# Reordering the loads and the plan of an eight-core transformer-layer kernel on Trainium2

## The reference, cut to what matters

```python
h   = modulate(layer_norm(x), mod_x[0], mod_x[1])          # mod = silu(c) @ w_ada + b_ada
q, k, v, u, vb, ga, gb = split(h @ w_in)
ya  = window_attention(rope(q), rope(k), v, kc, vc, sink)  # +-128 tokens, and 256 context keys
vn  = layer_norm(gelu(vb), gmlp_ln_g, gmlp_ln_b)           # per chunk of 128 tokens:
yb  = gelu(u) * (w_s @ vn + b_s)
mix = (sigmoid(ga) * (ya @ w_a) + sigmoid(gb) * (yb @ w_b)) @ w_o
x_mid = layer_norm(ALPHA * x + mod_x[2] * mix)             # then a SwiGLU FFN, and a second norm
```

## Time and profile before

| | us |
|---|---|
| median of 3 runs | 969.98 |
| lowest and highest run | 969.21, 974.94 |
| the profiled execution, slowest core and what lies around it | 974.86 |
| span of its slowest core (core 6) | 973.1 |
| PE busy in that span | 890.9 |

### The profile page before, as it was taken

One profiled execution on the slowest core, in us unless ns is written; L12 is line 12 of the kernel. 1 busy time (PEld: TensorE's weight loads), 2 busy tenths in 40 slices (PEclk: granted clock), 3 DMA queues, 4 the chain that ended last, 5 costly groups with the idle time before them and its releaser, 6 DMA issues.

```text
span 973.1 us, 15750 instructions; the slowest of 8 cores (966.4 to 973.1 us)
## 1 busy us (share of the span) xinstructions
PE 890.9 (92%) x5495; PEld 446.2 (46%) x5589; DVE 622.9 (64%) x1131; ACT 317.7 (33%) x494; POOL 284.6 (29%) x231
## 2 busy tenths in 40 slices
PE   1389688898999999999999999999999999999995
PEld 1235444344554444444444544444444444444673
DVE  4337686857655666766687476556656674666787
ACT  1436775546867243334435200111111001011110
POOL 6024263555554233324312540202202021111111
PEclk9999898979999999999999999999999999999999
DMA  8997622339963500026321480303213020111112
GB/s 203 202 187 190 174 87 66 88 46 161 164 95 81 174 1 1 1 88 100 114 47 44 173 192 25 87 1 87 36 52 87 0 44 1 44 44 57 52 66 87
DMA packets 30380, 83.91 MB, mean 86 GB/s; under 512 B 2912, under 2 KB 3168, under 8 KB 28640
## 3 DMA queue, kind: packets, MB, share of 16 engines
q0 software_dynamic: 18064, 34.54, 22.9%
q1 hardware_dynamic: 12240, 48.37, 14.2%
HBM read 109.05 MB, written 8.39 MB: 121 GB/s over the span
## 4 chain that ended last, share of the span: by engine, by line
PE 84%; DMA 6%; DVE 4%; issue 3%; ACT 2%; POOL 1%; DVEq 0%; POOLq 0%; SPq 0%; ACTq 0%
PE psum L1178 31%; PE psum L1204 15%; PE psum L1016 11%; PE psum L1033 6%; PE psum L1067 6%; DMA arena<-wqk 4%; PE psum L673 3%; PE psum L729 3%; PE psum L900 2%; PE psum L936 2%; PE psum L760 2%; DMA arena<-ctxb 1%; DVE arena L495 1%; PE psum L1102 1%; DVE arena L974 1%
## 5 line engine op out<-in xcount | busy, mean ns | idle before, releaser
L1178 PE MATMUL psum<-arena 128*128 128x512 bf16 (+1 forms) x1515 | 314.5, 361 | 1.1
L1178 PEld LDWEIGHTS psum<-arena 128*128 128x128 bf16 x1536 | 150.2, 98 | 154.5
L1184 ACT ACTIVATE arena<-psum 128x512 f32<-128x512 f32 (+1 forms) x96 | 53.9, 562 | 380.4 <-PE psum L1178 380.4
L1204 PE MATMUL psum<-arena 128*128 128x512 bf16 x681 | 161.0, 379 | 1.9 <-DVE arena L1187 0.7
L508 POOL TENSOR_TENSOR arena<-arena 128x1 f32<-128x1 f32 (+1 forms) x74 | 70.9, 958 | 287.2 <-DVE arena L506 272.0
L1218 DVE TENSOR_TENSOR arena<-arena,psum 128x512 f32<-128x512 f32 x224 | 140.5, 679 | 18.8 <-PE psum L1204 18.6
L1187 DVE TENSOR_TENSOR arena<-psum,arena 128x512 bf16<-128x512 f32 (+1 forms) x96 | 62.0, 646 | 131.2 <-PE psum L1178 127.8
L1016 PE MATMUL psum<-arena 128*128 128x512 bf16 x498 | 115.7, 379 | 1.4 <-issue 1.0
L495 DVE BATCH_NORM_STATS2 arena<-arena 128x6 f32<-128x512 f32 x152 | 99.7, 685 | 14.5 <-DMA arena<-xh 3.8
L1204 PEld LDWEIGHTS psum<-arena 128*128 128x128 bf16 x704 | 68.6, 98 | 82.7 <-issue 2.6
L906 ACT ACTIVATE arena<-psum 128x1024 bf16<-128x1024 f32 (+1 forms) x100 | 80.7, 852 | 23.2 <-PE psum L900 22.1
(11 more groups left out here) (95 smaller groups left out, 883.2 us busy)
## 6 DMA issues: line engine op xcount, KB each, us to landing
arena<-xh SPq DMA_DIRECT2D x34, 512.0 KB, 7.7
arena<-wada POOLq DMA_DIRECT2D x24, 512.0 KB, 18.0
arena<-wff POOLq DMA_DIRECT2D x11, 1024.0 KB, 9.2
arena<-wff SPq DMA_DIRECT2D x11, 1024.0 KB, 7.0
out<-arena SPq DMA_DIRECT2D x15, 512.0 KB, 2.6
arena<-wc POOLq DMA_DIRECT2D x8, 768.0 KB, 20.0
arena<-wout SPq DMA_DIRECT2D x8, 512.0 KB, 4.4
arena<-rope SPq DMA_DIRECT2D x4, 512.0 KB, 11.5
```

What stands on the lines that cost most here:

```text
L1178: ins = e.matmul(bank(ps)[:, 0:n], lhsT=w1v[r][:, k, lo:lo + 128], rhs=h2(k), start=(k == 0), stop=(k == 7))
L1184: s = P.op('act', prio - 150, act_cost(n), lambda e: e.activation(out=sgv(), in_=bank(pg)[:, 0:n], func=AF.Silu), after=[a], takes=[sg], g ...
L1204: ins = e.matmul(bank(ps), lhsT=actv[(r, fi, t)], rhs=w2v[r][:, fi, h * 512:(h + 1) * 512], start=(n == 0), stop=(n == 2 * len(rounds) - 1))
```

## The change: loads moved, a lag and costs raised, one wait added

It does this:

- The `w_ada` pieces 8 to 11 are no longer loaded behind `wvvb` into four buffers. Their loads wait for the second tile of group 3 and have two buffers.
- Tile buffers: two more, in the part of `qg` that belongs to group 3. Group 3's tiles may use them. (Buffers 6 and 7 of `a4` lie in the same place; pieces 8 to 11 no longer use them, so q and u of group 3 need not wait for those pieces.)
- The first rotation table is loaded behind piece 5 of `w_ada`. All that stands behind it on SP's queue follows it.
- The bias product on PE waits for the table `bsbc`.
- `LAG` of POOL goes from 0.12 to 1.2, and some costs go up, so that the whole order is made anew.
- A DVE instruction (`t_shut`) is added, whose result nothing reads: the branches `MASKPE` and `ZPOOL` are off.

```diff
-    LAG = {'pe': 0.24, 'act': 0.10, 'dve': 0.10, 'pool': 0.12, 'sp': 0.1}
+    LAG = {'pe': 0.24, 'act': 0.10, 'dve': 0.10, 'pool': 1.2, 'sp': 0.1}
...
-    o_xr = [o_wo + 4 * KB * i for i in range(4)] + [L['qg'] + 8 * KB, L['qg'] + 12 * KB, L['vn'] + 4 * KB]
+    o_xr = [o_wo + 4 * KB * i for i in range(4)] + [L['qg'] + 8 * KB, L['qg'] + 12 * KB, L['vn'] + 4 * KB,
+                                               L['qg'] + 24 * KB, L['qg'] + 28 * KB]
...
-    rope_load('0', 14, rope_d[0], 512, [])
+    rope_load('0', 14, rope_d[0], 512, [ada_ld[5]])
...
-            res.append(P.op('pool', prio - 40, (hi - lo) / 512.0 * 1.1 + 0.2, ...
+            res.append(P.op('pool', prio - 40, (hi - lo) / 512.0 * 1.3 + 0.2, ...
...
-            t_vn[j] = P.op(me, prio + i - 20, 0.75 if me == 'dve' else 1.3, ...
+            t_vn[j] = P.op(me, prio + i - 20, 0.9 if me == 'dve' else 1.5, ...
...
-    m1 = P.op('pe', 58, 0.7, fgl, after=[c1, c2, ld_wst], takes=[pg], gives=[gh])
+    m1 = P.op('pe', 58, 0.7, fgl, after=[c1, c2, ld_wst, ld_bsbc], takes=[pg], gives=[gh])
...
+    shut = V(U0 + 46 * KB, BF16, 4, 128)
+    t_shut = P.op('dve', 58.5, 0.4, lambda e: e.tensor_scalar(
+        out=shut, in0=masks, scalar1=-1.0, scalar2=1e30, op0=ALU.add, op1=ALU.mult), after=[ld_masks, c2])
...
-    norm_group('3', [xh[(13 + i) * 128:(14 + i) * 128, :] for i in range(4)], 64, [ld_wu[1]])
+    ld_x3 = norm_group('3', [xh[(13 + i) * 128:(14 + i) * 128, :] for i in range(4)], 64, [ld_wu[1]], ('act', 'act'), room=(7, 8, 0, 1, 2, 3))
...
-        ada(8 + n, [(2, 2 * n), (2, 2 * n + 1)], 30 + n, (0, 1, 6, 7), after=[ld_wvvb])
-    ada_mid = ada_last[8:]
+        ada(8 + n, [(2, 2 * n), (2, 2 * n + 1)], 30 + n, (0, 1), after=[ld_x3[1]])
...
-    proj_qk(3, 108, ada_mid)
-    proj_u(3, 110, ada_mid)
+    proj_qk(3, 108)
+    proj_u(3, 110)
...
-                ex = P.op(me, prio + n * 0.1, 1.0 if me == 'dve' else 2.1, ...
+                ex = P.op(me, prio + n * 0.1, 1.1 if me == 'dve' else 2.2, ...
...
-        t_yb[j] = P.op('dve', prio + 0.9, 0.8, ...
+        t_yb[j] = P.op('dve', prio + 0.9, 0.98, ...
```

More of the change, by code:

```diff
@@ L772, in proj_v @@
             r, st = stat(prio + i, [gvs], 512, [[ge]], EPS)
-            mi = minus(st, prio + i - 20, r)
-            z = P.op('act', prio + i - 20, 0.82, lambda e, st=st, gvs=gvs: e.activation(
-                out=gvs(), in_=gvs(), func=AF.Identity, scale=rstd_of(st), bias=minus_of(st)), after=[mi], gives=[st])
             me = 'dve' if i % 2 == 0 else 'pool'
-            t_vn[j] = P.op(me, prio + i - 20, 0.75 if me == 'dve' else 1.3, lambda e, gvs=gvs, j=j: e.tensor_tensor(
+            if me == 'dve' or not ZPOOL:
+                mi = minus(st, prio + i - 20, r)
+                z = P.op('act', prio + i - 20, 0.82, lambda e, st=st, gvs=gvs: e.activation(
+                    out=gvs(), in_=gvs(), func=AF.Identity, scale=rstd_of(st), bias=minus_of(st)), after=[mi], gives=[st])
+            else:
+                z = P.op('pool', prio + i - 20, 1.0, lambda e, st=st, gvs=gvs: e.tensor_scalar(
+                    out=gvs(), in0=gvs(), scalar1=mean_of(st), scalar2=rstd_of(st), op0=ALU.subtract, op1=ALU.mult),
+                    after=[r], gives=[st])
+            t_vn[j] = P.op(me, prio + i - 20, 0.9 if me == 'dve' else 1.5, lambda e, gvs=gvs, j=j: e.tensor_tensor(
                 out=vn[:, j, :], in0=gvs(), in1=glg, op=ALU.mult), after=[z, ld_gl, busy], gives=[gv])
@@ L892, in attend @@
             ptv = lambda pt=pt: V(o_pt[sid(pt)], BF16, 8, 128)
+            mi = None
+            if kd == 'w' and s != 1:
+                mi = (0 if j == 0 else 1) if s == 0 else (3 if j == NT - 1 else 2)
             ex = []
@@ L900, in f @@
                         ins = e.matmul(b[:, i * 512:(i + 1) * 512], lhsT=ks[x * 64:(x + 1) * 64, :],
-                                       rhs=qv[x * 64:(x + 1) * 64, :, jt * 128:(jt + 1) * 128], start=True, stop=True)
+                                       rhs=qv[x * 64:(x + 1) * 64, :, jt * 128:(jt + 1) * 128], start=True, stop=mi is None)
+                        if mi is not None:
+                            ins = e.matmul(b[:, i * 512:(i + 1) * 512], lhsT=ident,
+                                           rhs=shut[:, mi:mi + 1, :].to_broadcast([128, 4, 128]), start=False, stop=True)
                     return ins
-                mm = P.op('pe', prio + n * 0.1, 0.2 * len(kv), f, after=need + tile_q(j),
+                mm = P.op('pe', prio + n * 0.1, 0.42 if mi is not None and j < MASKPE else 0.2 * len(kv), f, after=need + tile_q(j) + ([t_shut] if mi is not None and j < MASKPE else []),
                           behind=[s_last, gelus[(1, 2, 3)[min(j // 2, 2)]]], takes=[sp])
@@ L911, in attend @@
             exps.append(mm)
-            if kd == 'w' and s != 1:
-                mi = (0 if j == 0 else 1) if s == 0 else (3 if j == NT - 1 else 2)
+            if mi is not None and j < MASKPE:
+                shut_done.append(mm)
+            elif mi is not None:
                 me = 'dve' if s == 2 and j >= 4 else 'pool'
-                ex = P.op(me, prio + n * 0.1, 1.0 if me == 'dve' else 2.1, lambda e, ptv=ptv, mi=mi: e.tensor_tensor(
+                ex = P.op(me, prio + n * 0.1, 1.1 if me == 'dve' else 2.2, lambda e, ptv=ptv, mi=mi: e.tensor_tensor(
                     out=ptv(), in0=ptv(), in1=masks[:, mi:mi + 1, :].to_broadcast([128, 8, 128]), op=ALU.mult),
```

19 lines of the change are left out of this document (12 added, 7 removed).

## The result

Beside one another on the same chips the changed kernel took 968.07 us and the kernel before 974.07, medians of 20 runs each; the ratio is 0.9944 [0.9931, 0.9957], 5.4 us less. The forecast was 9.6 less (960.4; range 951 to 972), counted from 969.98, the median of the 3 runs known then. In the profiled execution of the changed kernel, 968.28 us, core 7 is the slowest, with a span of 966.5.

What follows compares the result with a forecast made beforehand. PE was taken to bound the kernel, with gains only where it stands still or runs at 1.2 GHz; -7.6 - 1.0 - 1.0 = -9.6 us took 969.98 to 960.4, range 951 to 972.

Steps and rivals of the forecast that it cites:

- Gate pieces, -7.6: 97 to 117 us: with gate loads moved away, context tiles and `bsbc` land 7 us earlier; net -7.6 us.
- rival 3: Tiles don't come sooner, as when the plan holds back their buffers by the lag: 970 us; chance 0.03.
- The margin and the raised costs, 0: POOL's raised lag and costs only reorder the engines; 0 us, bounds -8 and +21.
- Rival 1: The new order is better after 117 us too: a further -8 us, 952; chance 0.16.
- Rotation tables, -1.0: Start, up to the first projection at 52.28: tables behind piece 5 spare `w_ada` pieces; -1.0 us net.
- Two tile buffers, -1.0: Two of group 3's tiles come ten us sooner, their statistics falling into DVE's idle time; -1.0 us.
- Bias wait, 0: PE's bias product waits in the open for `bsbc`; 0 us, range 0 to +1.8.
- gate pieces late, 0: Later gate pieces end near 119 us, 13 us of cover before `w_out` at 131.78; cost 0.
- Rival 2: From 117 us DVE can't keep up and takes back 6 to 7 us: 967; chance 0.17.
- Rival 4: Slower: raised lag puts POOL's masks and rotation sums on more DVE products, 117 to 240 us: 982; chance 0.10.

Runs made afterwards that it cites:

- 10: Changed kernel with two more buffers for normed copies, for the halo group alone; 0.9934 of the kernel before.
- run 12: Changed kernel with two of the halo group's four normed copies allowed on DVE instead of ACT; 1.0003 of the kernel before.
- run 3: Changed kernel with POOL's old lag of 0.12, raised costs kept; 0.9902 of the kernel before.
- run 7: Changed kernel with POOL's lag of 1.2 on all steps but the norms' powers, which have 0.12; 0.9943 of the kernel before.
- run 6: Changed kernel with POOL's lag of 1.2 only behind the norms' powers, 0.12 elsewhere; 0.9939 of the kernel before.
- run 4: Changed kernel with the four gate pieces issued early again, beside the halo and context tiles; 0.9991 of the kernel before.
- run 2: Changed kernel with old lag and old costs: moved loads, tile buffers and the bias product's wait kept; 0.9932 of the kernel before.
- run 1: Kernel before with only POOL's lag raised from 0.12 to 1.2; 0.995 of the kernel before.
- run 16: Kernel before with only the four raised costs of the change; 1.0014 of the kernel before.
- run 14: Changed kernel with POOL's lag at 0.12 and the bias product without its wait for its table; 0.9936 of the kernel before.
- run 9: Changed kernel with POOL's lag at 1.5 instead of 1.2; 0.9942 of the kernel before.
- 13: Changed kernel with POOL's lag at 0.12 and two of the halo group's four normed copies allowed on DVE; 0.9989 of the kernel before.
- 8: Changed kernel with POOL's lag at 0.6 instead of 1.2; 0.9915 of the kernel before.

## Why the prediction missed, step by step

**Gate pieces, -7.6: the step that failed.** "So the second context tile lands near 95.1 instead of 102.1, 7 us earlier" took the issue as given at 91.29 and the best time on the way, 3.8 us, for the rest. In the changed kernel it is issued at 91.74 and takes 6.35 us, so of the 3.0 us that are missing 2.5 lie on the way and 0.5 in the issue; with the lag off it is issued at 89.88 and takes 6.43, landing at 96.31. When it is issued hangs on ACT's copies of group 2, which I hadn't looked at: that is a part of the condition of rival 3, to which I gave 0.03. Then "moved up by 7 us they let the halo projection begin near 107 ..., so I leave 1.5 us of standstill". It moved by 4.0 us, just as the tile did, but the idle time before it was 5.87 + 1.62 + 1.30 and 1.09 at the bias product, 9.88 us, and 8.26 busy us at half clock cost 4.1 more. So "All four have one root: the context tiles and `bsbc` come late" did not hold: the tile landed 4.0 us sooner and `bsbc` 5.5 (98.87 against 104.33), and PE stood longer.

In front of the halo group stand ACT's modulations of group 2 and four copies in a row (10 and 12). And the lag took away what PE had to do meanwhile: the v projection of one tile that runs 3 and 7 have inside the gap stands ahead of it in the changed kernel and in 6, and the next one comes only at 120 us. That this cover, and not the halo group's way, makes the 5.1 us by which run 3 is ahead at 60 us of work can be read from all cores. The halo projection begins at 112.2 us in the changed kernel and at 112.3 in run 3 (medians), though the copies begin 1.7 us sooner in run 3. By then run 3 has done 53.5 us of work and the changed kernel 51.3: 2.2 us less, one tile's v projection. From there to 60 us run 3 needs 6.4 us for 6.5 of work, the changed kernel 11.6 for 8.7: the other 2.9 us fall where its clock is still at half (to 117.70 in the profile shown), while PE has no idle time from 117 us on.

That the pieces hold back the tiles, and these the halo group, was right: moving the pieces back costs 4.6 us with the lag and 12.6 without, and there 9.7 of the 12.6 are lost by 60 us of work, where the term was placed. With the lag they are lost after it: the halo projection of run 4 comes 7 us later, and yet at 60 us of work run 4 is ahead of the changed kernel, by 2.1.

**The margin and the raised costs, 0.** Right in the sum and wrong as a picture. Beside the loads they give 1.2 us away (0.9944 against 0.9932, not to be told from none). Inside, the lag takes 5.1 us up to 60 us of work (123.8 against 118.7 in run 3) and gives 3.2 back by 120. The trace of before has the rows that speak against 1.2, and I passed them by: DVE's `minus` begins 0.16 us after POOL's power has ended, as 0.35 are enough in run 3.

```profile
104.24 0.70 POOL L508 TENSOR_TENSOR arena<-arena 128x2 f32<-128x2 f32 x1 [1.97 <-DVE arena L525]
...
105.10 0.15 DVE L525 SCALAR_TENSOR_TENSOR arena<-arena 128x2 f32<-128x2 f32 x1
```

Rival 1, better order after 117 us, came true in part: from 60 to 120 us of work the changed kernel needs 72.8 us, the kernel before 79.0, 6.2 less of the 8 that it named. The lag alone does that too (72.2), the loads alone do 4.5 of it (74.5).

DVE's chunk product shows the collision with POOL less: its longest is 1.98 us (median 0.69), against the 4.30 of the earlier trace rows. It is 4.30 again in run 2 and 4.31 in run 6, 1.33 in run 7, 2.65 in run 1, and without any lag 2.07 in run 3, 2.61 in run 16 and 2.00 in run 14. First the changed kernel, then run 9 with its lag of 1.5 (core 0):

```profile
L994 DVE TENSOR_TENSOR arena<-arena x16: 674/692/1979, 103.0 to 238.0; 128x512 bf16<-128x512 f32 x16
```

```profile
L994 DVE TENSOR_TENSOR arena<-arena x16: 678/692/3921, 102.0 to 243.2; 128x512 bf16<-128x512 f32 x16
```

The Trainium skill ("SBUF — State Buffer", section "Who interferes with whom") has a DVE instruction with two SBUF inputs and a GpSimd instruction that reads SBUF exclude one another. That a margin behind GpSimd avoids this only by luck agrees: run 14 has no lag and a longest product like the changed kernel's, run 9 has the largest lag and one of 3.92 us. How long they are doesn't decide the time either: in run 3, 4 us faster than the changed kernel, 8 of the 16 products take over 0.8 us, in the changed kernel 4.

**Rotation tables, -1.0.** Right: the first projection comes at 51.09 against 52.28, and the first 5 us of work end 1.0 sooner. The gain and its return are both in the rows, as the prediction had it:

```profile
27.90 0.56 PE L468 MATMUL psum<-arena 128*128 128x2 bf16 x16 [1.86 <-DMA arena<-wada]
31.28 0.57 PE L468 MATMUL psum<-arena 128*128 128x2 bf16 x16 [2.82 <-DMA arena<-wada]
...
38.52 0.61 PE L468 MATMUL psum<-arena 128*128 128x2 bf16 x16
```

The fourth of these is 5.3 us ahead of its 43.78 of the earlier trace rows; the wait for `wqk` then rose from 2.05 to 4.43. The Trainium skill's rule that all queues share the DMA engines ("DMA: Bandwidth & Descriptors", section "Issuing engines are not separate DMA queues") would have made the term 0; most of the 5.3 us did go, and 1.2 were left at the first projection.

**Two tile buffers, -1.0.** Group 3's first statistics run at 103.63 instead of 113.70, as said, and 135 to 160 us has 4.2 us more of busy PE. What of this the buffers do wasn't tried apart, nor was the added DVE instruction.

**Bias wait, 0; gate pieces late, 0.** PE waits 1.09 us for the table, within the range given; run 14 shows no gain without it. The last gate product runs from 129.41 to 129.98, it doesn't end near 119, and `w_out` is issued at 132.27 against 131.78: the cover of 13 us held, with little left.

**The other rivals.** Rival 2, DVE taking the gain back, named 967, near what was measured, but from 117 to 135 us PE has no idle time in the changed kernel: it wasn't DVE here. Runs 12 and 13, slower again after 60 us of work and with PE waiting for DVE, are the case that it describes. Rival 4 didn't occur.

**The sum.** All loads together were put at -9.6 and measured at -6.6 (run 2). The best of what was run is the change without the lag (3; with 0.6, as 8): 0.9902 [0.9864, 0.994], 4 us below the changed kernel by the medians' ratio, though the intervals touch. What stays open: why most orders made with a lag, and that of the loads alone, run better from 123 to 200 us (the half clock and the stalls differ in all of them), and whether the lag's size has an optimum.

## What to carry to other kernels

When a transfer seems late, look at both of its parts: who lets it be issued, and how long it is then on its way. Here SP's wait named ACT, and no relief among the transfers makes SP issue a tile sooner; and the way stayed 2.5 us longer than the best one seen before. Where a planner orders the engines, a margin isn't free: here it drew independent work ahead of a chain that runs through the engine, so that none was left to cover the chain's wait. Price single parts of such a change by their own runs, but don't add them up, since each remakes the order: here 6.6 and 4.9 us made 5.4.

## What the runs showed of the hardware

How long the half clock (0.50, the 1.2 GHz level) lasts between 94 and 124 us, by the clock records of all eight cores: 6.8 to 10.2 us in the kernel before, 13.7 to 17.1 in the changed one, 3.4 to 10.2 in run 3. Neither the longest stall of PE nor the sum of its stalls of over 1 us orders it alone. On the profiled cores it was 3.41 us with a longest stall of 2.75 and a sum of 6.2 (run 3), 6.83 with 2.40 and 7.8 (before), 10.24 with 4.58 and 5.9 (run 14), 13.65 with 2.06 and 6.9 (run 16), 17.07 with 3.71 and 8.2 (run 12), and 13.65 to 17.07 with 5.6 to 5.9 and some 10 (changed, 6, 10). Over all cores of all runs the half clock goes with the sum somewhat better than with the longest stall (correlations 0.72 and 0.54, my working from the 144 cores): a tendency, no rule.

In price: 13.65 us at half clock held 8.26 busy us in the changed kernel, so 4.1 are the clock's; the 3.41 of run 3 held 3.23, so 1.6.
